# Feed-forward gated tile transposed by VectorE in 32x32 blocks and a round trip through device memory; forget gates as the stationary operand

## The reference, cut to what matters

```python
def swiglu(n, w_gate, w_up, w_down):
    return (jax.nn.silu(n @ w_gate) * (n @ w_up)) @ w_down
...
z = h @ w_in[l]
q_r, k_r, v_r, gt_r, q_f, k_f, v_f, f_f, a_r, a_f = split_cols(z)
...
log_f = jax.nn.log_sigmoid(f_f.astype(jnp.float32) + b_forget[l].astype(jnp.float32))
```

## Time and profile before

| | us |
|---|---|
| median of 3 runs | 1378.33 (1377.07 to 1378.73) |
| the profiled execution's own time | 1376.84 |
| its span | 1375.1 |
| TensorE busy | 1366.6 |
| VectorE busy | 853.6 |
| ScalarE busy | 774.4 |
| bytes moved by DMA | 251.57 MB, mean 183 GB/s |

### The profile page before, as it was taken

The page is one execution under the profiler, slowest core; times in us unless marked ns, Lnnn a source line. Parts: engine busy times, 40 slices in busy tenths (PEclk is TensorE's granted clock), DMA queues, the critical chain, the costliest instruction groups (busy, mean ns, idle before and its releaser), DMA issues.

```text
span 1375.1 us, 19419 instructions
## 1 busy us (share of the span) xinstructions
PE 1366.6 (99%) x6466; PEld 1135.6 (83%) x6466; DVE 853.6 (62%) x1350; ACT 774.4 (56%) x1251; POOL 50.0 (4%) x86
## 2 busy tenths in 40 slices
PE   9999999999999999999999999999999999999999
PEld 7888888888888888888888888888888888888887
DVE  6655556767655557755556676555566756665553
ACT  6555556645655546655556675555566675655552
POOL 1000010000000001000001010000002000000000
PEclk9999999999999999999999999999999999999999
DMA  8766626665666654766663347666455654575560
GB/s 292 233 205 218 214 92 203 214 202 169 199 200 204 191 176 138 229 195 189 190 198 100 120 134 240 204 190 186 152 144 179 201 169 138 168 230 183 185 209 33
DMA packets 198292, 251.57 MB, mean 183 GB/s; under 512 B 17922, under 2 KB 136928, under 8 KB 198240
## 3 DMA queue, kind: packets, MB, share of 16 engines
q1 hardware_dynamic: 197968, 250.86, 57.9%
q0 software_dynamic: 224, 0.03, 0.0%
q10 hardware_dynamic: 48, 0.02, 0.0%
HBM read 249.80 MB, written 1.05 MB: 182 GB/s over the span
## 4 chain that ended last, share of the span: by engine, by line
PE 95%; DVE 2%; ACT 1%; issue 1%; DMA 0%; SPq 0%; POOL 0%; DVEq 0%; ACTq 0%
PE ps L1933 30%; PE ps L1935 30%; PE ps L1934 29%; PE ps L1959 2%; PE ps L2072 2%; DMA raw<-in_ffn_w_up 0%; PE ps L2236 0%; PE ps L2588 0%; PE ps L2416 0%; PE ps L2417 0%; ACT whi L610 0%; DVE wlo L1226 0%; PE ps L2263 0%; POOL stat L586 0%; SPq L334 0%
## 5 line engine op out<-in xcount | busy, mean ns | idle before, releaser
L1223 DVE SCALAR_TENSOR_TENSOR wlo<-raw,gcol,whi 128x512 fp32r<-128x512 f32 x592 | 413.8, 746 | 274.0 <-ACT whi L610 273.9
L1933 PE MATMUL ps<-whi,kthi 128*128 128x512 f32 (+2 forms) x1384 | 548.4, 396 | 1.4 <-DVE wlo L1223 1.1
L1935 PE MATMUL ps<-whi,ktlo 128*128 128x512 f32 (+2 forms) x1384 | 537.1, 388 | 0.0
L1934 PE MATMUL ps<-wlo,kthi 128*128 128x512 f32 (+2 forms) x1384 | 536.3, 388 | 0.0
L610 ACT ACTIVATE whi<-raw,gcol 128x512 fp32r<-128x512 f32 x592 | 392.2, 714 | 228.5 <-PE ps L1935 223.2
L1935 PEld LDWEIGHTS ps<-whi,ktlo 128*128 128x128 f32 x1384 | 259.8, 188 | 54.3
L1933 PEld LDWEIGHTS ps<-whi,kthi 128*128 128x128 f32 x1384 | 260.0, 188 | 54.0 <-issue 1.9
L1934 PEld LDWEIGHTS ps<-wlo,kthi 128*128 128x128 f32 x1384 | 260.3, 188 | 48.9
L1231 DVE TENSOR_TENSOR wlo<-raw,whi 128x1024 fp32r<-128x1024 f32 x140 | 169.9, 1223 | 108.7 <-ACT whi L614 108.3
L614 ACT CAST whi<-raw 128x1024 fp32r<-128x1024 f32 x140 | 145.5, 1050 | 129.8 <-PE ps L1935 129.8
L1933 PE MATMUL ps<-whi,hthi 128*128 128x512 f32 x400 | 156.0, 390 | 0.0
(11 more groups left out here) (243 smaller groups left out, 807.2 us busy)
## 6 DMA issues: line engine op xcount, KB each, us to landing
raw<-in_ffn_w_gate SPq DMA_DIRECT2D x176, 256.0 KB, 2.9
raw<-in_ffn_w_up SPq DMA_DIRECT2D x176, 256.0 KB, 3.1
raw<-in_ffn_w_down SPq DMA_DIRECT2D x160, 256.0 KB, 3.4
raw<-in_w_in SPq DMA_DIRECT2D x80, 256.0 KB, 3.4
raw<-in_gmlp_w_in SPq DMA_DIRECT2D x64, 256.0 KB, 3.2
raw<-in_w_gate SPq DMA_DIRECT2D x44, 256.0 KB, 2.8
raw<-in_w_up SPq DMA_DIRECT2D x44, 256.0 KB, 3.1
raw<-in_w_down SPq DMA_DIRECT2D x40, 256.0 KB, 3.3
```

Source lines behind the costliest of these rows:

```text
L1223: ins = nc.vector.scalar_tensor_tensor(out=wlo[:, s, cut], in0=raw[:, s, cut], scalar=gcol[:, k:k + 1], in1=f32(whi[:, s, cut]), op0=ALU.m ...
L1933: nc.tensor.matmul(dst, lhs[0], rhs[0], start=first, stop=False)
L1934: nc.tensor.matmul(dst, lhs[0], rhs[1], start=False, stop=False)
L1935: return nc.tensor.matmul(dst, lhs[1], rhs[0], start=False, stop=last)
```

## The change

In the loop and for the first tile of each part, the four transposes on TensorE go. VectorE transposes `hid` in blocks of 32x32, with two instructions, into the left half of `sq_out`, arranged so that each partition holds its row contiguous. SyncE writes that half to a scratch tensor in device memory with one DMA of 256 KB, waits for it, and reads it back with four DMAs of 64 KB (32 partitions each, pieces of 512 bytes), which put the blocks on their partitions in the right half of `sq_out`. ScalarE and VectorE make `hthi` and `htlo` from there and no longer from bank 6. TensorE now waits for the gated tile itself before it writes banks 4 and 5 again. The last tile of each part is transposed on TensorE as before.

For the forget gates the 16 columns become the stationary operand and the 256 tokens the moving one: 16 matmuls of 256 columns, whose result is then copied by ScalarE and turned by two small transposes in the middle of tile 3.

```diff
+        hid_dram = nc.dram_tensor("hid_dram", [P, TT * FT], F32, kind="Internal").ap()
+        hid_blocks, hid_moved = sq_out[:, 0:TT * FT], sq_out[:, TT * FT:2 * TT * FT]
...
+            def hid_out(n):
+
+                sp.wait_ge(sem("hid_turned"), n)
+                sp.dma_start(hid_dram, hid_blocks).then_inc(sem("hid_out"), 16)
+
+            def hid_in(n):
+
+                sp.wait_ge(sem("hid_out"), n * 16)
+                for j in range(4):
+                    sp.dma_start(hid_moved[32 * j:32 * j + 32, :].rearrange("p (i x) -> p i x", i=4),
+                                 hid_dram.rearrange("(i p) (j x) -> j p i x", i=4, j=4)[j]).then_inc(sem("hid_moved"), 16)
...
-                        for s in range(4):
+                        for s in range(3):
                             gate_up(s, j + ahead[s], gate, up, j * FT + FT)
-                        for f in range(2):
-                            rows(4 + f, j + behind[f], down, j * 2 + f)
+                        hid_out(j + ffns[0] * (NF - 1))
+                        gate_up(3, j + ahead[3], gate, up, j * FT + FT)
+                        rows(4, j + behind[0], down, j * 2)
+                        hid_in(j + ffns[0] * (NF - 1))
+                        rows(5, j + behind[1], down, j * 2 + 1)
...
                 def turned_hidden(j):
 
-                    act.wait_ge(sem("hid_full"), j + (b + 1))
-                    nc.scalar.copy(hthi[:].rearrange("p c n -> p (c n)"), ps[:, 6, :]).then_inc(sem("ht_high"), 1)
+                    act.wait_ge(sem("hid_moved"), j * 64 + (moved * 64 + 64))
+                    nc.scalar.copy(hthi[:].rearrange("p c (t i x) -> p (c t) i x", t=2, i=4),
+                                   hid_moved.rearrange("p (i ct x) -> p ct i x", i=4, ct=4)).then_inc(sem("ht_high"), 1)
...
+            def hid_turn(n):
+
+                dve.wait_ge(sem("hid_ready"), n)
+                for t in range(TT):
+                    out = hid_blocks.rearrange("p (j c t x) -> p t c j x", j=4, c=2, t=2)[:, t]
+                    ins = nc.vector.transpose(out, hid[:, t, :].rearrange("p (c j x) -> p c j x", c=2, j=4))
+                ins.then_inc(sem("hid_turned"), 1)
...
                     for t in range(TT):
                         gated_tile(t, pre, j * 2 + (b + t + 1))
+                    hid_turn(j * 2 + (b + 2))
                     low(3, j + base[3], name)
...
-                def hid_flip(j):
-
-                    pe.wait_ge(sem("hid_ready"), j * 2 + (b + 2))
-                    for t in range(TT):
-                        ins = hid_turn(6, t, lambda c: c * S + t * P)
-                    ins.then_inc(sem("hid_full"), 1)
-
...
                 with pe.Fori(2, NF - 1) as j:
+                    pe.wait_ge(sem("hid_ready"), j * 2 + b)
                     tile_product(lambda s: j + base[s])
                     down(j - 1)
-                    hid_flip(j)
...
-            def forget_gates(c, t):
-                narrow = ps[:, t, 0:8], ktlo[:, c, t * P:t * P + P], f_high_low[:, c, 0:8]
-                both = ps[:, t, 0:16], kthi[:, c, t * P:t * P + P], f_high_low[:, c, :]
...
+            def forget_gates(c):
+                nc.tensor.matmul(ps[0:16, 0, 0:S], f_high_low[:, c, :], kthi[:, c, :], start=c == 0, stop=False)
+                ins = nc.tensor.matmul(ps[0:8, 0, 0:S], f_high_low[:, c, 0:8], ktlo[:, c, :], start=False, stop=c == KC - 1)
...
+            def turn_gates():
+                pe.wait_ge(sem("f_read"), 1)
+                for t in range(TT):
+                    ins = nc.tensor.transpose(ps[:, 1, 16 * t:16 * t + 16], f_t[:, t * P:(t + 1) * P], ident[0:16, 0:16])
+                ins.then_inc(sem("f_turned"), 1)
...
-            mix2_tile(3)
+            mix2_tile(3, between=turn_gates)
```

80 lines of the change are left out of this document (43 added, 37 removed).

## The result

The changed kernel takes 1427.6 us in the median of four runs (1416.2 to 1428.7), the kernel before 1377.8 us: a ratio of 1.034, 95% interval 1.029 to 1.039. It is slower, where 1365 us had been forecast. Here is its page: TensorE, the chain, three groups of instructions (busy us and mean ns, then the idle time before them) and the DMA issues (us to landing).

A forecast was written before the change was run, and what follows sets the result against it. TensorE was taken as the bound. Transposes removed -24.5 us, forget gates -1.7, waits at first tiles +10.7, last tiles +2: -13.5 us, giving 1365 us against a median of 1378.33; range 1356 to 1394.

The forecast's parts named there:

- The cycle: Loop from one ScalarE copy into `hthi` to the next, through memory and not TensorE: 15.6 us against TensorE's 16.32.
- Steps 1 and 2: From the copy to VectorE's first low part, 1.37 us; then low parts of slots 0 to 2 and gated tile, 4.85.
- step 3: Two block transposes of 128x256 on VectorE: 0.70 us for both, bounds 0.35 and 1.40.
- steps 4, 5 and 6: Low parts of slots 3 and 4, 2.46 us; SyncE's issues until the last read, 2.65; that read's landing, 2.9.
- hidden up to a landing of 3.4: The write to memory, needing 0.2 + 2.1 us, lies beside other work that gives it 3.6 us.
- step 6: The last 64 KB read from issue to landing: 2.9 us, bounds 2.1 and 5.0.
- the first rival: The round trip sets the pace and TensorE waits in every tile: 1417 us at a cycle of 17.0; chance 0.27.
- The likeliest case: A cycle between 15 and 16 us with waits at the starts of parts: 1358 to 1372 us; chance 0.53.
- 4.1 us wait at ffn10: TensorE's wait for `htlo` at the start of the third part, reads standing behind slot 4's loads: 4.1 us.
- the 1.4 at the second part: TensorE's wait for `htlo` before the first down product of the second part: 1.4 us.
- just fits: The trip at a part's last tile: 10.4 us beside a half tile of 10.9; 0.4 us a part allowed.
- The added work costs nothing beyond the cycle: VectorE's extra 0.7 us and the extra 0.5 MB of traffic a tile add no time of their own.

The follow-up runs named there:

- E12: The change with write and reads issued earlier, later slots for the turned tile, the trip only for tiles 1 to 8, tile 0 in its old place: 1356.4 us.
- E1: The kernel before with only the stationary forget gates, nothing of the round trip: 1376.2 us against 1377.2, ratio 0.9993.
- E3: The change without its write; the four reads wait for the turn and fetch rows of a weight: 1410.4 us, ratio 1.025.
- E9: The change with an eighth of the bytes in every weight load of the loops, same transfers and places: 1361.2 us, ratio 0.988.
- E11: The change with the reads alone moved ahead of slot 3's load and the down rows, right behind the write: 1374.0 us, ratio 0.998.
- E4: The change with the write ahead of the loads of slots 1 and 2 and the reads ahead of slot 3's: 1374.3 us, ratio 0.9975.
- E2: The change with TensorE's transposes back and used; VectorE's turns, the write and the reads still made but unused: 1377.0 us, ratio 0.9997.
- E10: The change with the write alone moved ahead of the loads of slots 1 and 2, the reads left in place: 1522.9 us, ratio 1.104.
- E6: The change with write and reads issued earlier on SyncE, and the turned tile's high and low parts behind slots 0 and 1: 1366.0 us, ratio 0.993.

## Why the prediction was wrong

**What bounds the kernel, and what is removed: right.** TensorE's 16.32 us a tile without its transposes appear to the hundredth in E12's steps, and its span agrees with the terms to 0.8 us. The forget gates, forecast at 1.7 us, were worth 0.9 in E1's time and 1.2 in its trace.

**The cycle: the mechanism right, its part under way mis-sized, and with it the side on which it ends.** Steps 1 and 2 were as forecast, step 3 0.77 us for two turns in place of 0.70 (0.42 each in the groups, overlapping). From the turn to the landing of the last read the forecast had steps 4, 5 and 6, 2.46 + 2.65 + 2.9 = 8.0 us; it was 9.3. What failed in the kernel as it ran is the sentence that the write is "hidden up to a landing of 3.4": the write needed 4.8 us, so that the reads went out 4.9 us after the turn and not 3.6, and the last of them was issued 6.2 us after it and not 5.1. That is 1.1 of the 1.3 us; step 6, the last read, took 3.1 us where 2.9 stood. But step 6 is mis-sized too, for the case in which the write is hidden: take the write away, and the reads go out at the 3.6 us of the forecast and the last takes 4.3 (E3), 9.4 us in all again. The 2.9 nearly held in the change only because the queue stood still for the write meanwhile, with nothing new issued. So the one mistake is to price each transfer by a single row of its size, and not by what stands ahead of it. What counts is how much is in the engines ahead of the last read (E9, E11): three slots' loads go out in the 4 us before the turn and two more before the reads, and the engines then are 97% busy.

The write's price, 2.1 us, came from stores with no loads beside them. The read's did not: the engines were full around that row too, and the same view of the kernel before has a second read of 64 KB, issued 0.48 us after it, which the prediction doesn't show. It is the next line, and below it stands the window of the first one (DMA share and GB/s last):

```profile
hid<-in_c_ones SPq DMA_DIRECT2D x1, 64.0 KB, 4.3
1016.00:1019.00 3.00, 3.00 (x15) 2.49 (x14) 0.75 (x2) 1.22 (x2) 0.00 (x0) 1.00 0.92 284
```

With 4.3 in step 6 the sum would have been 17.0 us. The loads that landed after 5.0 us in the densest stretch pointed the same way. I named them as the upper bound and as what spoke for the first rival ("the pattern of the stretch with 5.0 us landings") and set against it the mean rate of 183 GB/s, which is an average over stages with different limits.

**"The margin is only 0.7 us in 15.6."** The cycle was 17.0 us in the median and 17.5 in the turn shown. The likeliest case needed a sum of seven terms to hold within 5%; 0.27 for the rival was too little for that. Its own numbers were near: a cycle of 17.0, 27 us in the loops (measured 33), 10.7 + 7 at the starts (18) and 20 at the ends (14), 1417 us; the profiled run took 1416.2, the median 1427.6. The nearness is in part luck: the rival put the 1.4 us into the landing of the read, where in the change most of it was the write.

**Starts and ends.** The 4.1 us wait at ffn10 was 5.1, and the 1.4 at the second part 2.6; there too the write landed late, after 5.0 and 5.1 us. At ffn10 it also stood behind other loads on the queue: it was issued 13.4 us after its turn and landed 1.3 us after slot 4's issues, for which alone the forecast had the reads wait. The ends were forecast at 0.4 us a part for a trip that "just fits"; TensorE stood 1.8 to 3.1 us there, although the last trip, with nothing ahead of it, is the quickest: its reads go out 2.03 us after the write, and in four of the five parts the copy comes 5.3 to 5.5 us after the turn. It seems to have been late because the tile before it was: in E4, with the loops in step, this wait is gone in four of the five parts.

**The added work costs nothing beyond the cycle: right** (E2).

**What was left out.** The lower clock after long waits, 5 us of TensorE's time in the change; it was among the signs, not in a sum. How much of it reaches the total was not measured. In E10 180 steps stand at the lower clock, 36 us more of TensorE's time than at the upper one, and yet the steps stay those of the cycle, 19.5 us, which does not run through TensorE.

**What stays open:** why the unprofiled runs of the change took 7 to 12 us more than the profiled one, and E6's spread of 8 us. In both the cycle or the starts hang on landings, which may differ from run to run; E12, where nothing waits for them, spreads by 0.6 us. That is an argument, not shown.
